# A two-layer hybrid backbone on one core: layer 1's routing gathers before it weighs, and a modulation chunk and two loads are placed anew between the layers

## The reference, cut to what matters

```python
def grouped_moe(h, router_w, router_bias, w_gate, w_up, w_down):
    scores = jax.nn.sigmoid((h @ router_w).astype(jnp.float32))
    sel = scores + router_bias.astype(jnp.float32)
    grp_score = lax.top_k(sel.reshape(-1, N_GROUPS, EXPERTS_PER_GROUP), 2)[0].sum(-1)
    best = jnp.argmax(grp_score, axis=-1)
    in_group = (jnp.arange(N_EXPERTS) // EXPERTS_PER_GROUP)[None, :] == best[:, None]
    _, idx = lax.top_k(jnp.where(in_group, sel, -jnp.inf), TOP_K)
    w = jnp.take_along_axis(scores, idx, axis=-1)
    w = w / jnp.sum(w, axis=-1, keepdims=True)
    gates = jnp.sum(jax.nn.one_hot(idx, N_EXPERTS, dtype=jnp.float32) * w[..., None], axis=1)
    ...
    y = (jax.nn.silu(h @ w_gate[e]) * (h @ w_up[e])) @ w_down[e]
    out = out + gates[:, e:e + 1].astype(h.dtype) * y
```

## Time and profile before

| | |
|---|---|
| three runs | 967.47, 970.38, 971.39 us; median 970.38 |
| profiled execution | 969.95 us, of which the span of its trace is 968.1 us |
| PE busy | 902.3 us (93%) |
| DVE, ACT, POOL busy | 387.6, 258.0, 115.9 us |
| mean granted clock of TensorE | 0.982 of full speed |
| HBM read and written | 299.35 and 14.47 MB, 324 GB/s over the span |

### The profile page before, as it was taken

How to read it: one execution, slowest core, us unless ns; L and a number is a source line. 1 busy time by engine, 2 the same in 40 slices (tenths; PEclk the granted TensorE clock), 3 DMA queues, 4 the chain that set the end, 5 groups by cost and what they waited for, 6 DMA issues and landing times.

```text
span 968.1 us, 14234 instructions
## 1 busy us (share of the span) xinstructions
PE 902.3 (93%) x5142; PEld 470.5 (49%) x5143; DVE 387.6 (40%) x829; ACT 258.0 (27%) x418; POOL 115.9 (12%) x226
## 2 busy tenths in 40 slices
PE   3899999999979999999999969999988999999996
PEld 0444434343436656565656615447534544555453
DVE  2379999943662222222222234476353111111112
ACT  2413546432421111111112122046231111111112
POOL 2300000100021111111111130000002111011110
PEclk9999999999979999999999978999999999999999
DMA  9992397577488999989999994484467999999994
GB/s 350 349 380 92 139 379 264 180 269 291 172 335 343 423 425 424 421 321 419 382 427 423 394 338 154 178 312 184 174 226 267 422 418 424 424 421 428 423 425 167
DMA packets 68308, 314.32 MB, mean 325 GB/s; under 512 B 4668, under 2 KB 5088, under 8 KB 51888
## 3 DMA queue, kind: packets, MB, share of 16 engines
q1 hardware_dynamic: 54608, 275.78, 71.7%
q0 software_dynamic: 8992, 29.75, 8.3%
q10 hardware_dynamic: 4672, 8.30, 2.3%
HBM read 299.35 MB, written 14.47 MB: 324 GB/s over the span
## 4 chain that ended last, share of the span: by engine, by line
PE 83%; DVE 7%; DMA 4%; issue 2%; ACT 2%; SPq 2%; POOL 0%; ACTq 0%; DVEq 0%; POOLq 0%
PE ps L795 27%; PE ps L808 14%; PE ps L575 10%; PE ps L611 7%; PE ps L772 3%; PE ps L865 3%; PE ps L903 3%; PE ps L496 2%; DMA weight_ring<-in_ev_w_in 2%; PE ps L763 2%; SPq L362 2%; DVE arena L1096 2%; PE ps L804 2%; PE ps L943 1%; PE ps L595 1%
## 5 line engine op out<-in xcount | busy, mean ns | idle before, releaser
L795 PE MATMUL ps<-weight_ring,arena 128*64 128x256 f32 x1792 | 199.0, 380 | 5.0 <-issue 3.6
L795 PEld LDWEIGHTS ps<-weight_ring,arena 128*64 128x64 f32 x1792 | 140.2, 137 | 71.0 <-issue 20.2
L1393 DVE TENSOR_TENSOR arena<-arena,ps 128x128 f32<-128x128 f32 x78 | 19.0, 284 | 248.5 <-PE ps L795 248.5
L575 PE MATMUL ps<-hT,weight_ring 128*128 128x512 f32 x256 | 115.2, 605 | 2.0 <-DMA weight_ring<-in_ev_w_in 2.0
L808 PE MATMUL ps<-weight_ring,arena 128*64 128x512 f32 x448 | 102.3, 597 | 2.5 <-DVE arena L1406 0.2
L1096 DVE SCALAR_TENSOR_TENSOR arena<-arena,par 128x512 f32<-128x512 f32 x132 | 95.0, 750 | 5.5 <-PE ps L575 1.0
L1804 ACT ACT_TABLE_LOAD x39 | 50.0, 1283 | 129.8 <-issue 129.5
L575 PEld LDWEIGHTS ps<-hT,weight_ring 128*128 128x128 f32 x256 | 48.0, 192 | 66.3 <-issue 61.2
L795 PE MATMUL ps<-arena 128*64 128x256 f32 x704 | 78.0, 379 | 0.0
L611 PE MATMUL ps<-weight_ring,arena 128*128 128x512 f32 x160 | 70.8, 595 | 0.7 <-DVE arena L1543 0.5
L795 PEld LDWEIGHTS ps<-arena 128*64 128x64 f32 x704 | 56.2, 137 | 24.5 <-issue 5.9
(11 more groups left out here) (331 smaller groups left out, 915.3 us busy)
## 6 DMA issues: line engine op xcount, KB each, us to landing
weight_ring<-in_ada_w SPq DMA_DIRECT2D x24, 2048.0 KB, 14.9
weight_ring<-in_exp_w_gate SPq DMA_DIRECT2D x22, 2048.0 KB, 10.3
weight_ring<-in_exp_w_up SPq DMA_DIRECT2D x22, 2048.0 KB, 10.5
weight_ring<-in_exp_w_down SPq DMA_DIRECT2D x22, 2048.0 KB, 10.8
arena<-in_exp_w_gate SPq DMA_DIRECT2D x10, 2048.0 KB, 10.5
hT<-in_exp_w_down SPq DMA_DIRECT2D x10, 2048.0 KB, 10.8
arena<-in_exp_w_up SPq DMA_DIRECT2D x10, 2048.0 KB, 10.7
weight_ring<-in_ev_w_in SPq DMA_DIRECT2D x4, 2048.0 KB, 20.2
```

What stands on the lines that cost most here:

```text
L575: last = mm(ps[:, m % 4, :], wide(slot)[:, k, P * j:P * j + P], hT[:, k, :], start=(k == 0), stop=(k == KD - 1))
L795: last = mm(ps[64 * fh:64 * fh + 64, bank, 0:256], xgT[:, k % 4, 64 * (k // 4):64 * (k // 4) + 64], w[:, k, 256 * fh:256 * fh + 256], star ...
```

## The change

Between the layers:
- `GAP_ADA` is 3 and not 4: chunk ada 9 is multiplied (L487) after the second of the four token tiles of qkv 2, its columns are transposed after the third, its sum is taken on VectorE after the third tile's copy, and ScalarE reads it behind the second half of the modulated columns. PE takes the chunks in the order in which they are loaded, so `USE` goes.
- The load of qkv 2 (slot 0) waits for `s_yg[1]`, the second upper gather. The wait for `s_yg[3]` now stands ahead of ada 9 and not of qkv 0.
- VectorE takes the gap's three sums behind the first and third lower add and the first upper add. ScalarE loads its table for the square root ahead of the last of the three reads.

In the routing:
- Layer 1 uses layer 0's way: bf16 one-hots without a third group, gates after the indices, a product of their own (`slot_gates(1, 3)`, into bank 3, behind the transposes of the first tile and ahead of its products), and a widening of the slot one-hots on ScalarE.
- In both layers the tile's start comes out of two scalings and not three, and the copy of the tile numbers goes; the product reads them with one more broadcast dimension.
- `residual_rows(7)` of layer 1 moves behind the product of the one-hots.

```diff
-GAP_ADA = 4
+GAP_ADA = 3
-USE = [0, 1, 2, 4, 3] + list(range(5, len(MID)))
@@ SP
+                if kind != "ada" and slot == 0 and count[slot] == pre_n[slot]:
+                    sp.wait_ge(s_yg[1], 16)
                 if sum(count) - sum(pre_n) == GAP_ADA + 1:
                     sp.wait_ge(s_yg[NT - 1], 16)
@@ PE, router and experts
                 if l:
                     residual_rows(6)
-                    residual_rows(7)
...
                 ada_columns(3)
                 if l:
                     residual_rows(5)
+                    residual_rows(7)
                     bounds = first_bounds(l)
                     pe.wait_ge(s_mods, 6)
                     tr(ps[0:8, 2, 0:P], mods[:, 1, 8 * G2:8 * G2 + 8, LAT], ident[:, :]).then_inc(s_modT, 1)
-                    pe.wait_ge(s_gt[1], 1)
                     residual_rows(4)
...
+            def slot_gates(l, bank):
+                m = 2 * len(toks(l))
+                pe.wait_ge(s_wide, l + 1)
+                pe.wait_ge(s_gt[l], 1)
+                for i in range(m):
+                    last = mm(ps[:, bank, 0:GMAX], oh_wide[l][:, i, :], oh_gate[l][:, i, :], start=(i == 0), stop=(i == m - 1))
+                last.then_inc(s_id, 1)
...
                 tile_transposes(l, 1, 0, 4)
+                if l:
+                    slot_gates(1, 3)
@@ PE, projection
                 if t == 1:
                     half_ready(KD - 1, 1)
+                    ada_product(5)
+                if t == 2:
+                    ada_columns(7)
@@ VectorE, routing
-                link(v.tensor_scalar(t64, hl, 1.0 / MT, -(MT - 1) / (2.0 * MT), ALU.mult, ALU.add))
-                link(v.tensor_scalar(t64, t64, ROUND, None, ALU.add))
-                link(v.tensor_scalar(t64, t64, -ROUND, float(MT), ALU.add, ALU.mult))
+                link(v.tensor_scalar(t64, hl, -(MT - 1) / 2.0, ROUND * MT, ALU.add, ALU.add))
+                link(v.tensor_scalar(t64, t64, -ROUND * MT, None, ALU.add))
...
-                link(v.tensor_copy(tn.rearrange("p (c t) -> p c t", c=2), tile_no[:, :, 0:n]))
-                if l:
-                    choice_gates()
-                    for c in range(2):
-                        v.tensor_tensor(oh_tile(l)[:, n * c:n * c + n, 2, :], ...)
...
+                choice_gates()
+                for c in range(2):
+                    last = v.tensor_tensor(oh_gate[l][:, n * c:n * c + n, :], i3[:, n * c:n * c + n, :], ...)
+                    link(last)
                 dve.sem_inc(s_gt[l], 1)
...
+                else:
+                    dve.wait_ge(s_id, 4)
+                    link(v.tensor_copy(slot_tab[:, :, 1], ps[:, 3, 0:GMAX]))
@@ ScalarE
+                    act.wait_ge(s_oh, 2)
+                    s.activation(oh_wide[1], oh_slot(1), ACT.Copy).then_inc(s_wide, 1)
...
-            for _ in range(GAP_ADA):
+            for n in range(GAP_ADA):
+                if n == GAP_ADA - 1:
+                    s.activation(att[:, 3, 1:2], epsc[:, 0:1], ACT.Sqrt)
                 ada_read(5)
...
             modulate_half(1)
+            ada_read(5)
```

More of the change, by code:

```diff
@@ L210, in build @@
         fing = reg(12576, D)
-        oh_wide = wbd.rearrange("p g d j o -> p (g d j o)").rearrange("p (i s) -> p i s", i=2 * NT)
         after_lru = wbd.rearrange("p g d j o -> p (g d j o)")
+        oh_wide = [after_lru[:, at:2 * NT * P].rearrange("p (i s) -> p i s", s=P) for at in (0, NT * P)]
         iota_tok, spread = after_lru[:, 0:SEQ], after_lru[:, SEQ:2 * SEQ]
@@ L346, in build @@
         OH_GATE = 3600
-        oh_gate = rt(0, OH_GATE, 2 * NT * GMAX).rearrange("p (i g) -> p i g", g=GMAX)
+        oh_gate = [rt(l, at, 2 * len(toks(l)) * GMAX).rearrange("p (i g) -> p i g", g=GMAX)
+                   for l, at in ((0, OH_GATE), (1, 848))]
         def summed(i):
@@ L475, in next_chunk @@
             def next_chunk():
-                slot = MID_SLOT[USE[state["chunk"]]]
+                slot = MID_SLOT[state["chunk"]]
                 state["chunk"] += 1
@@ L727, in router @@
                     residual_rows(6)
-                    residual_rows(7)
                 pe.wait_ge(s_oh, l + 1)
                 for i in range(2 * n):
-                    last = mm(ps[:, 4, 0:(2 + l) * GMAX], oh_slot(l)[:, i, :], oh_tile(l)[:, i, :, :].rearrange("p w g -> p (w g)"),
+                    last = mm(ps[:, 4, 0:2 * GMAX], oh_slot(l)[:, i, :], oh_tile(l)[:, i, :, :].rearrange("p w g -> p (w g)"),
                               start=(i == 0), stop=(i == 2 * n - 1))
@@ L747, in router @@
                     ada_columns(3)
[L748 to L752, removed]
-                return bounds
+                    slot_gates(0, 5)
+                return bounds
+            def slot_gates(l, bank):
[5 more added lines that the diff above has]
+                last.then_inc(s_id, 1)
             def tile_transposes(l, count, k0, k1):
@@ L1363, in route @@
                     sum_columns(1, 3)
-                    choice_gates()
-                    for c in range(2):
-                        last = v.tensor_tensor(oh_gate[:, n * c:n * c + n, :], i3[:, n * c:n * c + n, :],
-                                               gates2[:, c, 0:n].unsqueeze(2).to_broadcast([P, n, GMAX]), ALU.mult)
-                        link(last)
+                choice_gates()
+                for c in range(2):
+                    last = v.tensor_tensor(oh_gate[l][:, n * c:n * c + n, :], i3[:, n * c:n * c + n, :],
+                                           gates2[:, c, 0:n].unsqueeze(2).to_broadcast([P, n, GMAX]), ALU.mult)
+                    link(last)
                 dve.sem_inc(s_gt[l], 1)
@@ L1435, in _ @@
             for i in range(NT):
[L1436 removed]
+                if i % 2:
                     sum_columns(1)
@@ L1451, in _ @@
                 v.tensor_copy(kv[:, t, :], ps[:, t, :]).then_inc(s_qkve, 1)
+                if t == 2:
+                    sum_columns(1)
             link(add_bias(1, 6, 10))
```

16 lines of the change are left out of this document (4 added, 12 removed).

## The result

| | before | after |
|---|---|---|
| median of the comparison, 20 runs each (us) | 970.88 | 975.55 |
| lowest and highest | 967.47, 978.02 | 971.84, 981.46 |
| profiled execution, and its span | 969.95, 968.1 | 976.65, 974.9 |
| PE busy | 902.3 | 903.1 |

After over before is 1.0038, 95% interval 1.0023 to 1.0053. The changed kernel is slower, by less than the 0.5% that the prediction called no change, and 13 us above the predicted 962.3. The direction was wrong.

The account below looks back on a forecast made before the run. The prediction took the passage between the layers to be bound by a full transfer system, not an engine. 969.95 - 0.4 (routing 0) - 4.9 (passage) - 2.8 (routing 1) = 961.9 profiled, median 962.3; range 958.5 to 967.5.

Parts of the forecast that it names:

- Step 1: Between the layers: the fourth lower gather lands 3.7 us after issue, about 562.9; the four adds end at 568.2.
- Step 2: Between the layers: last stores land in 2.7 us, first upper gather is issued at 564.5, upper gathers land in 4.0.
- Step 3: Between the layers: gap's third columns done at 569.5, table load costs nothing, transposes at 574.2, columns ready about 577.9.
- Step 4: Held qkv 2, issued at 569.7, lands about 579; projection from 579.0 instead of 586.53, -7.5 us.
- rival B: Between the layers: gathers are slow by themselves, not through the loads, so held qkv 2 starts late; 976; chance 0.04.
- Step 5: Behind the projection's second tile: one moved product and its columns now lie in a PE-bound stretch, +2.6 us.
- Routing 0: Layer 0's routing: the same two small operations less ahead of the one-hots, -0.4 us (bounds 0 and -0.5).
- C: Layer 1's routing: register loads or the gates' products hold PE; gain 1.0 instead of 2.8, 964.1; chance 0.10.
- D: Layer 1's experts: the weight stream takes the gain; 2% slower costs 2.2 us net, 964.5; chance 0.04.
- E: Between the layers: TensorE stays at 2.4 GHz, load lands as early as columns; projection at 576, 959.3; chance 0.10.
- part 2: Layer 1's routing: indices and gather 3.0 us earlier, transposes 2.9 earlier; -2.8 us in all (bounds -1.3 and -3.1).
- A: Between the layers: two gathers and qkv 2 slow each other; projection at 583, total -4.1, 966.3; chance 0.15.

Follow-up runs that it names:

- e7: Before with the passage change alone, less the four gathers of the lower experts' rows; one run, span 967.7 us.
- e4: Before with the passage change alone, but the load of qkv 2 not held for the second upper gather; ratio to before 0.9998.
- e5: After, with layer 1's load of expert 1's down weights held for the first tile's gather and qkv 2 not held; ratio to before 0.9964.
- e1: Before with the change between the layers alone, routing as before; ratio to before 1.0010.
- e11: After, with only VectorE's wait for the gate row moved into the loop, ahead of the product that reads it; ratio to before 1.0028.
- e9: e5 with VectorE's wait for the gate row moved into the loop, ahead of the product that reads it; ratio to before 0.9965.
- e10: Before with both routing changes, expert 1's down-weights load held for the first tile's gather, and the gate row's wait moved into the loop; ratio to before 0.9966.
- e2: Before with the change in the routing of both layers alone, passage as before; ratio to before 1.0001.
- e3: After, with layer 1's load of expert 1's down weights held until the first tile's gather has landed; ratio to before 0.9995.
- e8: Before, with only layer 1's load of expert 1's down weights held until the first tile's gather has landed; ratio to before 1.0046.

## Why the prediction was wrong

**Step 1, lower gathers: half right.** The adds start at 565.65, not 563 or 570. The gathers took 6.2 us from the issue of the fourth, between the bounds; I took the lower bound. It did no harm by itself: the stores came later still.

**Step 2, upper gathers: the step that failed first.** I let the last stores land in 2.7 us and the gathers in 4.0. The stores took 5.10, since the lower gathers were still on their way (2.24 without them, e7). The gathers took about 5.4, and the second still 5.14 with nothing but its own kind in flight (e7): in after it landed at 574.6, not 569.7. Two terms, 2.6 and 1.4 us, plus 0.9 for a first issue on POOL that lasted 1.85 us. The slip was to price both from a system that the change was to make quiet, and then to leave out what the change leaves in it: the lower gathers beside the stores, and the four upper gathers beside each other.

**Step 3, engines: right in what it says of them.** The transposes started at 578.75, as much later than my 574.2 as the gathers were late. The product and its columns in the gap and the table load never showed as the late one, though the third product took 3.47 us at the low clock and not 1.92.

**Step 4, the new wait: wrong by 6.5 us, and the mechanism was rival B's.** qkv 2 went out at 574.66 instead of 569.7 and needed 10.84 us instead of about 9, beside two gathers and then the loads of chunk 9 and qkv 0 and 1, which the sum took to have no part in it. The landing of the gather makes 4.9 of the 6.5 us, the load 1.5. Projection 585.54 instead of 579.0: -1.0 and not -7.5 against before. B said that the gathers are slow by themselves and not through the loads, and that the held load then starts too late. The first is shown in that they stay slow with no load in flight (e7). The second is shown in that PE waits 1.71 to 3.48 us for the load where it is held and does not where it is free (e4, e5). I had given it 4 in 100 and, with it, a price of +5.7 in all through a landing in 17.9. But 585.54 is still earlier than the 587.1 from which B called the kernel slower: by B's own account, with the gains that it counted elsewhere, the kernel would have come out 1.6 us ahead of before. That it came out slower took two things more, the low clock in the first tile and the loss in routing 1. B's chance should have been much larger. The prediction says that nothing shows a gather of this size in a quiet system, and let one of half the size speak for it; before's own last upper gather, 5.24 us with no load beside it, was there to be read.

**Step 5, what moves behind: size right, and one term missing.** The product took 1.85 and the columns 0.44. But the first projection tile ran 8.53 us instead of 7.53, at the low clock behind the 3.48 us of idle. With this and the product, -1.2 at the projection's start against the gap's became +2.3 at its end. The passage was forecast at -4.9 and came out at +2.3 in the profiled pair. The same code gives -0.8 in e1, whose gap started at 561.04, where the old passage is shorter too, and -1.0 in e11, whose gap started at 558.71. So part of after's value is this execution's; none of the four traces with this passage comes near -4.9.

**Routing 1: the vector and PE arithmetic was right, the gather's cover was not seen.** Forecast: one-hots' product 2.9 us earlier (measured 2.90), its length 0.3 to 0.64 (0.30), indices and gather 3.0 earlier (3.7). The step that failed is "Indices and gather come 3.0 earlier ... I take 2.9": it took the gather's 3.7 us as a constant. It is 3.4 with no load beside it and 7.35 beside the load it had been running behind by luck. The transposes came out 0.2 later instead of 2.9 earlier. Between them and the tile, where the gates' product was to add 0.1 to 0.2, 1.3 were added at the low clock, and the first products took 1.5 more. So the stretch came out at +2.9 instead of -2.8. That the -2.8 itself is real is shown by e9 and e10 (-3.7 and -3.0), once the load is held and the gate row's wait no longer stands ahead of the loop. The slot gates took 0.98 at full clock; they cost nothing that shows in e9.

**Routing 0: -0.4 forecast, nothing found.** The first tile of layer 0 started at 284.30 and not 285.69, but its first products took 8.81 us instead of 7.13, since the clock had fallen to 1.2 GHz, so the first down product came at 294.31 against 294.01. PE's timeline of after:

```profile
284.30 8.81 PE L799 MATMUL ps<-weight_ring,arena 128*64 128x256 f32 x64 [0.69 <-ACT arena L1804]
```

That first down product lies anywhere from 292.9 to 298.3 over the 14 traces, unchanged code included, by where the clock falls. No edit of 0.4 us can be read there.

**Rivals C and D.** C had PE held by register loads or by the gates' products; those are in nobody's way (e9). D, the weight stream, took nothing in after: 207.80 against 207.72 us over the loop, though its slack is gone. In e2, e4 and e10 PE does wait for weights, 0.33 to 0.55 us at a time near the end, and the loops are 208.2, 208.8 and 208.3 us long.

**The range.** By the terms given, E with part 2 at its bound is 959.0 and A with part 2 at -1.3 is 967.8, not 958.5 and 967.5; the measured 975.55 lies outside either way.

**What is shown and what is not.** Shown: that the load beside the gather costs routing 1 its gain (e3), that a second cover lay behind it (e8, e9), that the held qkv 2 makes PE wait (e4, e5), that four gathers of this size are slow without any load beside them (e7). Not shown: that the +2.9 and +2.3 us of the two stretches are the change's in every execution; e7 has the first without the new routing, and e11 lacks the second with the new passage. Not settled: how the +3.7 us of the median divides. e1 and e2 alone are at 1.0010 and 1.0001, and by their intervals the sum of the two could be anything from -3 to +5 us.

## What to carry to other kernels

Before you issue a small transfer earlier, look at which big load is in flight at the new instant and not at the old one: its landing time is no constant, and a neighbour that is released by something else will not move with it. Where the path hangs on a transfer, a wait that holds a big load back pays only if the next small transfer, and every wait placed ahead of its need, is clear of that load too. And a load that is not late today should not be made to wait for a transfer that is: the two landings then add up. Last, when several transfers of one kind go out in a row, price one of them from a row where they ran in a row, not from one that ran alone.

## What the runs showed of the hardware

A 2 MB load took 7.5 us nearly alone (before), 10.2 beside gathers of 256 KB (after), and 9.1 to 10.8 beside gathers of 512 KB and later loads (e11, after). A gather of 256 KB took 3.4 us with no load beside it (e3) and 6.4 to 7.35 beside a load issued 3.0 us ahead of it (e11, after). Of four gathers of 512 KB in a row with no load in flight the second took 5.14 us, and from 568 to 572 they moved 299 GB/s with the engines used to 93% (e7).

TensorE's clock fell to 1.2 GHz behind idles of 2.85 to 3.9 us for the gather, but not only there: in after it fell ahead of layer 0's first tile behind idles of 1.02 and 0.69 us, and in e7 ahead of layer 1's behind 1.89 us, with the code of before, which kept its clock at that place. What a fall costs varied: the tile's first 64 products took 7.13 us at full clock and 8.60, 9.55, 9.58 and 9.71 in after, e2, e11 and e7.
